# Expert passes of 32 rows in four column strips, three experts' rows at once, nine weight slots

## What is computed

```python
def hier_moe(x, w_group, b_group, w_router, b_router, w_gate_up, w_down):
    ...   # top-1 of 4 groups, then top-2 of the 8 experts in that group
    order = jnp.argsort(expert)
    ...
    def expert_block(a):
        xb, e = a
        gate, up = jnp.split(xb @ w_gate_up[e], 2, axis=-1)
        return (jax.nn.silu(gate) * up) @ w_down[e]
    ...   # sum of each token's two rows with their weights
```

## Time and profile before

| what | value |
|---|---|
| median of the runs shown | 2142.19 us |
| the profiled execution, its own time | 2152.84 us |
| its span, first to last instruction | 2150.9 us |
| TensorE (PE) busy | 1699.6 us, 79% |
| VectorE (DVE), ScalarE (ACT), POOL busy | 487.9, 324.3, 121.9 us |
| bytes read from and written to HBM | 551.57 MB, 52.01 MB |
| mean granted TensorE clock | 0.905 of full speed |

### The profile page before, as it was taken

The page is one execution under the profiler, slowest core; times in us unless marked ns, Lnnn a source line. Parts: engine busy times, 40 slices in busy tenths (PEclk is TensorE's granted clock), DMA queues, the critical chain, the costliest instruction groups (busy, mean ns, idle before and its releaser), DMA issues.

```text
span 2150.9 us, 25298 instructions
## 1 busy us (share of the span) xinstructions
PE 1699.6 (79%) x8325; PEld 783.4 (36%) x8326; DVE 487.9 (23%) x1022; ACT 324.3 (15%) x601; POOL 121.9 (6%) x147
## 2 busy tenths in 40 slices
PE   5988687687947888787887679989748788788682
PEld 3433233345432433333332334434523333233231
DVE  1679344320150101000000132120410000000003
ACT  3022334222020000001110220000200011010001
...
DMA  9951586685047596999999930201468899999995
GB/s 353 416 172 70 204 306 235 228 301 227 0 161 311 214 414 259 401 419 417 423 423 420 350 139 0 79 0 41 195 243 329 324 416 422 421 423 422 421 423 214
DMA packets 144964, 604.27 MB, mean 281 GB/s; under 512 B 15952, under 2 KB 18289, under 8 KB 128362
## 3 DMA queue, kind: packets, MB, share of 16 engines
...
HBM read 551.57 MB, written 52.01 MB: 281 GB/s over the span
## 4 chain that ended last, share of the span: by engine, by line
PE 63%; DMA 12%; DVE 10%; issue 7%; ACT 4%; POOL 1%; SPq 1%; ACTq 1%; DVEq 0%; POOLq 0%
PE ps L883 19%; PE ps L896 10%; PE ps L1008 8%; DMA ring<-in_w_gate_up_dram 5%; PE ps L578 5%; PE ps L594 3%; DMA ring<-in_w_down_dram 2%; PE ps L928 2%; PE ps L623 2%; PE ps L906 1%; DVE W L1483 1%; PE ps L940 1%; PE ps L520 1%; PE ps L496 1%; PE ps L718 1%
## 5 line engine op out<-in xcount | busy, mean ns | idle before, releaser
L883 PE MATMUL ps<-ring,W 128*64 128x512 f32 x2048 | 474.6, 615 | 48.3 <-issue 33.2
L896 PE MATMUL ps<-ring,W 128*64 128x512 f32 x1024 | 263.1, 659 | 54.7 <-DVE W L1806 49.3
L883 PEld LDWEIGHTS ps<-ring,W 128*64 128x64 f32 x2048 | 175.8, 141 | 335.1 <-issue 335.1
L1033 ACT ACTIVATE W<-ps 128x512 f32<-128x512 f32 (+3 forms) x244 | 138.1, 579 | 899.1 <-PE ps L896 353.8
L1800 DVE TENSOR_TENSOR W<-W,ps 128x256 f32<-128x256 f32 x64 | 27.0, 422 | 788.9 <-ACT W L1334 788.9
L1008 PE MATMUL ps<-hT,ring 128*128 128x512 f32 x384 | 168.0, 597 | 0.0
L896 PEld LDWEIGHTS ps<-ring,W 128*64 128x64 f32 x1024 | 88.0, 151 | 188.3 <-issue 188.2
L1008 PEld LDWEIGHTS ps<-hT,ring 128*128 128x128 f32 x384 | 72.8, 191 | 94.5 <-issue 94.5
L623 PE MATMUL ps<-ring,hT 128*128 128x512 f32 x192 | 88.6, 618 | 1.9 <-DVE W L1498 1.9
L1334 ACT ACTIVATE W<-ps 128x256 f32<-128x256 f32 x64 | 24.6, 384 | 423.3 <-PE ps L883 423.1
L1483 DVE SCALAR_TENSOR_TENSOR W<-W,prm 128x512 f32<-128x512 f32 x116 | 85.3, 805 | 0.0
...
## 6 DMA issues: line engine op xcount, KB each, us to landing
ring<-in_w_gate_up_dram SPq DMA_DIRECT2D x128, 2048.0 KB, 15.8
...
W<-x_rows SPq DMA_DIRECT2D x32, 512.0 KB, 15.4
x_rows<-W ACTq DMA_DIRECT2D x128, 128.0 KB, 6.7
...
```

The lines of the kernel that those rows point to most:

```text
L883: x = mm(ps[CAP * z:CAP * z + CAP, 2 + j, :], xt[:, k, :], at[:, :, 256 * z:256 * z + 256], start=(k == 0), stop=(k == KD - 1))
L896: x = mm(ps[CAP * z:CAP * z + CAP, 5 + j, :], ht[:, k % 2, CAP * (k // 2):CAP * (k // 2) + CAP], ring[:, 3 * j + 2, at:at + 512], start=(k ...
L1033: return fn(out, src, ACT.Copy, **k)
```

## The change

- `CAP` is 32. `x_rows` has 33 blocks of 32 rows ahead of the further area (`NEAR`), and every pass, main or further, has the form of today's further pass: stationary operands of 32 rows, four column strips, moving pieces of 256, one transpose between, a copy of 128 columns. An expert with more than 32 rows has a further pass for each 32 beyond.
- The rows of three experts (96) are loaded and turned at once, on ACT's queue instead of SP's, into one tile instead of two, a group ahead.
- The ring has nine slots. The three new ones lie over `hT` and a part of `W`, which for that become one tensor `M_` with `Hb`; the work tiles of the stage move into `Hb` (and `xg2` into free rows of `X`), and the router's tables move within `W`. Slots 6 and 7 are loaded once the logits are done, slot 8 once the bounds are. Loads then run three experts ahead.
- A loop body has three experts; two are written out behind it. A result is stored by four DMAs of 32 KB.

```diff
-CAP = 64
+CAP = 32
...
-PAIRS = E // 2
+GROUPS = -(-E // 3)
+NEAR = (E + 1) * CAP
 XTRA = 2 * (2 * T // XC)
-XR = -(-(E * CAP + (XTRA + NB - 1) * XC) // P) * P
+XR = -(-(NEAR + (XTRA + NB - 1) * XC) // P) * P
...
 NSLOT = 6
+NRING = 9
...
+M_SLOT = (M_HT, M_HT + SLOT, M_HT + 2 * SLOT)
...
-        Hb = sb("Hb", [P, NT, D])
-        hT = sb("hT", [P, KD, T])
-        W = sb("W", [P, W_N])
+        M_ = sb("M", [P, M_W + W_N])
+        Hb = M_[:, M_HB:M_HT].rearrange("p (a b) -> p a b", a=NT)
+        hT = M_[:, M_HT:M_W].rearrange("p (c t) -> p c t", c=KD)
+        W = M_[:, M_W:M_W + W_N]
...
+        xg, xT = m(M_XG, D)[0:3 * CAP], m(M_XT, KD, 3 * CAP)
+        hh, hhT, yh = m(M_HH, 3, P), m(M_HHT, 3, 4, CAP), m(M_Y, 3, 256)
...
+        def slot(s):
+            return ring[:, s, :] if s < NSLOT else M_[:, M_SLOT[s - NSLOT]:M_SLOT[s - NSLOT] + SLOT]
...
-        AHEAD = 2
+        AHEAD = 3
...
-            def quad(q, last=False):
-                step(4 * q, 0, 2 * q, 0)
-                step(4 * q + 1, 1, 2 * q, 0, nxt=(1, q, 2 * q + 1))
-                step(4 * q + 2, 0, 2 * q + 1, 1)
-                step(4 * q + 3, 1, 2 * q + 1, 1, nxt=None if last else (0, q + 1, 2 * q + 2))
-
-            with eng.Fori(0, E // 4 - 1) as q:
-                quad(q)
-            quad(E // 4 - 1, last=True)
+            with eng.Fori(0, E // 3) as q:
+                for j in range(3):
+                    step(3 * q + j, j, q, more=True)
+            for j in range(E % 3):
+                step(E - E % 3 + j, j, E // 3)
...
+                    sp.dma_start(slot(3 * j + k).rearrange("p (k n) -> p k n", k=4), src).then_inc(
...
-                def rows_in(p, j):
-                    sp.wait_ge(M["xt_mm"], pdone(l, p - 2))
-                    sp.dma_start(xg[:, j, :], x_dram[bass.ds(P * p, P), :]).then_inc(x_in[j], 16)
-
-                def step(n, j, e, pair=None):
-                    sp.wait_ge(M["g0_mm"], done(l, n))
-                    part(e, j, 0)
-                    sp.wait_ge(M["gu_mm"], done(l, n))
-                    part(e, j, 1)
-                    if pair is not None:
-                        rows_in(*pair)
-                    sp.wait_ge(M["down_mm"], done(l, n))
-                    part(e, j, 2)
-
-                layer_wait(sp, l, "disp", 32 * NT)
-                rows_in(0, 0)
-                rows_in(1, 1)
-                step(0, 0, 2 * EG, pair=(2, 0))
-
-                def quad(q, last=False):
-                    step(4 * q + 1, 1, 3 * EG + q)
-                    step(4 * q + 2, 0, q + 1, pair=(2 * q + 3, 1))
-                    step(4 * q + 3, 1, EG + q + 1)
-                    step(4 * q + 4, 0, 2 * EG + q + 1, pair=None if last else (2 * q + 4, 0))
-
-                with sp.Fori(0, 6) as q:
-                    quad(q)
-                quad(6, last=True)
-                step(E - 3, 1, E - 1)
+                layer_wait(sp, l, "h_ok", NT)
+                layer_wait(sp, l, "lg_mm", 1)
+                part(2 * EG, 2, 0)
+                part(2 * EG, 2, 1)
+                layer_wait(sp, l, "bounds", 1)
+                part(2 * EG, 2, 2)
+
+                def step(q, i):
+                    n, e = 12 * q + i, EG * ((i + 3) % G) + 3 * q + (i + 3) // G
+                    for k, name in enumerate(("g0_mm", "gu_mm", "down_mm")):
+                        sp.wait_ge(M[name], done(l, n))
+                        part(e, i % 3, k)
+
+                with sp.Fori(0, 2) as q:
+                    for i in range(12):
+                        step(q, i)
+                for i in range(E - 3 - 24):
+                    step(2, i)
...
-                def gate_up(xt, j, half, signal):
+                def gate_up(xt, j, half):
                     for k in range(4 * half, 4 * half + 4):
-                        at = ring[:, 3 * j + half, D * (k % 4):D * (k % 4) + D].rearrange("p (g f) -> p g f", g=2)
-                        for z in range(2):
-                            x = mm(ps[CAP * z:CAP * z + CAP, 2 + j, :], xt[:, k, :], at[:, :, 256 * z:256 * z + 256],
+                        at = slot(3 * j + half)[:, D * (k % 4):D * (k % 4) + D].rearrange("p (g f) -> p g f", g=2)
+                        for z in range(4):
+                            x = mm(ps[CAP * z:CAP * z + CAP, 2 + j, 0:256], xt[:, k, :], at[:, :, P * z:P * z + P],
                                    start=(k == 0), stop=(k == KD - 1))
-                    x.then_inc(signal, 1)
-
-                def h_turns(src, j, signal):
-                    for k in range(2):
-                        x = tr(ps[:, 4 + 3 * j, P * k:P * k + P], src[:, P * k:P * k + P], ident)
-                    x.then_inc(signal, 1)
-
-                def down(ht, j, signal):
+                    return x
+
+                def h_turn(src, j):
+                    return tr(ps[:, 2 + j, 256:256 + P], src, ident)
+
+                def down(ht, j):
                     for k in range(FE // P):
-                        for z in range(2):
-                            at = D * k + 512 * z
-                            x = mm(ps[CAP * z:CAP * z + CAP, 5 + j, :], ht[:, k % 2, CAP * (k // 2):CAP * (k // 2) + CAP],
-                                   ring[:, 3 * j + 2, at:at + 512], start=(k == 0), stop=(k == FE // P - 1))
-                    x.then_inc(signal, 1)
-
...
+                def group_turns(q):
+                    pe.wait_ge(x_in, q * 16 + (16 * GROUPS * l + 16))
+                    pe.wait_ge(M["xa_ok"], gdone(l, q - 1))
+                    pe.wait_ge(M["xd_ok"], gdone(l, q - 1))
                     carry(pe)
+                    n = 3 * CAP
                     for k in range(KD):
...
+                        x = tr(ps[:, k // 4, n * (k % 4):n * (k % 4) + n], xg[:, k:D:KD], ident[0:n, 0:n])
                     x.then_inc(M["xt_mm"], 1)
 
...
+                def step(n, j, q, more=False):
+
+                    def landed(k):
+                        pe.wait_ge(slot_in[3 * j + k], q * 16 + (base_in[l][3 * j + k] + 16))
+
...
                     further(pe, l, n, one_pass, ways=(2, 2, 2, 2))
-                    pe.wait_ge(M["xa_ok"], pdone(l, p))
-                    pe.wait_ge(M["xd_ok"], pdone(l, p))
-                    pe.wait_ge(M["h_ok"], done(l, n - 2))
-                    xt = xT[:, lane, :, CAP * j:CAP * j + CAP]
-                    landed(j, 0, p)
+                    if j == 0:
+                        pe.wait_ge(M["xa_ok"], gdone(l, q))
+                        pe.wait_ge(M["xd_ok"], gdone(l, q))
+                    pe.wait_ge(M["h_ok"], done(l, n - 3))
+                    xt = xT[:, :, CAP * j:CAP * j + CAP]
+                    landed(0)
                     carry(pe)
-                    gate_up(xt, j, 0, M["g0_mm"])
-                    landed(j, 1, p)
+                    gate_up(xt, j, 0).then_inc(M["g0_mm"], 1)
+                    landed(1)
                     carry(pe)
-                    gate_up(xt, j, 1, M["gu_mm"])
-                    if nxt is not None:
-                        pair_turns(*nxt)
+                    gate_up(xt, j, 1).then_inc(M["gu_mm"], 1)
+                    if more and j == 2:
+                        group_turns(q + 1)
                     pe.wait_ge(M["h_ok"], done(l, n))
-                    pe.wait_ge(M["ht_ok"], done(l, n - 2))
+                    pe.wait_ge(M["ht_ok"], done(l, n - 3))
                     carry(pe)
-                    h_turns(hh[:, j, :], j, M["ht_mm"])
-                    landed(j, 2, p)
+                    h_turn(hh[:, j, :], j).then_inc(M["ht_mm"], 1)
+                    landed(2)
                     pe.wait_ge(M["ht_ok"], done(l, n))
-                    pe.wait_ge(M["y_ok"], done(l, n - 2))
+                    pe.wait_ge(M["y_ok"], done(l, n - 3))
                     carry(pe)
-                    down(hhT[:, j], j, M["down_mm"])
-
-                pair_turns(0, 0, 0)
+                    down(hhT[:, j], j).then_inc(M["down_mm"], 1)
+
+                group_turns(0)
                 each_expert(pe, step)
...
+                def rows_in(q):
+                    act.dma_start(xg, x_dram[bass.ds(3 * CAP * q, 3 * CAP), :]).then_inc(x_in, 16)
...
+                gates(l, "gate2", w(W_G2, D), w(W_G2S, D, rows=NS), 0)
+                layer_wait(act, l, "disp", 32 * NT)
+                rows_in(0)
...
+                def group_turned(q):
+                    act.wait_ge(M["xt_mm"], gdone(l, q))
+                    act.wait_ge(M["gu_mm"], done(l, 3 * q - 1))
                     carry(act)
-                    copy(flat(xT[:, lane, 0:4, :]), ps[:, 0, :]).then_inc(M["xa_ok"], 1)
-
-                def step(n, j, p, lane, nxt=None):
+                    copy(flat(xT[:, 0:4, :]), ps[:, 0, 0:12 * CAP]).then_inc(M["xa_ok"], 1)
+
+                def step(n, j, q, more=False):
...
+                    if more and j == 0:
+                        carry(act)
+                        rows_in(q + 1)
                     further(act, l, n, one_pass)
```

(20 more changed lines are left out.)

169 lines of the change are left out of this document (81 added, 88 removed).

## The result

The changed kernel takes 2230.99 us (median of 4 runs, 2224.38 to 2252.32) against 2143.42 us on the same chip: a ratio of 1.041, 95% interval 1.034 to 1.049. It is slower, and the forecast of 2101 us (2063 to 2134) missed by 130 us. The profiled execution is the slowest of the four (2252.32 us, span 2250.6 against 2150.9), so its stretches are about 20 us longer in sum than the median's.

The account below looks back on a forecast made before the run. The prediction took the expert stages to be bound by the transfer of weights, with four stalls. Its terms, 30 + 8 + 11 - 4 + 0 - 4 = 41 us, taken from the median of 2142.19, gave 2101 us, range 2063 to 2134.

Parts of the forecast that it names:

- C, the stalls: Transfer standing still behind experts with further passes: 18 us won in layer 0, 7 lost in layer 1, sum +11 us.
- Pass of 8.94 us: Time of one further pass on TensorE, read from the kernel before and used for all 41 passes.
- 2 us of issue per cluster, nothing ahead of it: TensorE's idle time between an expert's last further pass and its main pass: 2.04 us in the profile before.
- Main pass of 7.6 us: Time of an expert's 32-row main pass on TensorE after the change: 7.2 us plus a share of turns, 7.6 us.
- A, nine slots: Three more weight slots filled during the router, taking 15.1 us per layer off the saturated transfer: +30 us.
- B: Fewer rows moved but shorter store pieces in the expert stages: between -7 and +22 us, taken as +8.
- E and F: Moved and new waits around the expert stages, such as dispatch, row gathers and projection: 0 and -4 us.
- D, the tail of layer 1: From last weights landing to last product: 15 to 16 us against 8, -8; with layer 0's +4, sum -4 us.
- E, the dispatch at 0: Start of the expert stages: first slot +2 us per layer, dispatch ending 2 us later beside slot 8, together 0.
- Slower: the clock: Rival: TensorE in the expert stages partly at half clock; 2185 us if a third of its work is; chance 0.08.
- The passes get dearer: Rival: row gathers beside weights make each further pass 2.5 us dearer, 40 us in all; 2141 us, chance 0.14.
- It doesn't do what it says: Rival: the three new slots don't fill ahead of the stage because SP waits earlier; 2131 us, chance 0.03.

Follow-up runs that it names:

- e2: The kernel before without its further passes (rows of an expert beyond 64 left out): 2069.5 us, ratio 0.962.
- e13: Kernel before with nine slots, still 64-row main passes, loop body of three experts, a one-cell Silu heading each body, three row buffers: 2177.4 us, ratio 1.012.
- e15: Changed kernel with a one-cell Silu at the loop body's head and ten empty loop turns on TensorE behind each cluster of passes: 2302.3 us, ratio 1.069.
- e5: Changed kernel with a one-cell Silu on ACT at the head of the loop body, so the table is loaded there: 2182.9 us, ratio 1.012.
- e1: Changed kernel without its further passes (rows of an expert beyond 32 left out): 2012.7 us, ratio 0.939.
- e18: Changed kernel without further passes, weights loaded two experts ahead instead of three, third set of slots not filled during the router: 2030.8 us, ratio 0.941.
- e12: Changed kernel with a one-cell Silu at the body's head and TensorE's four nested pass loops of two made two of four: 2182.8 us, ratio 1.013.
- e16: The kernel before with a one-cell Silu on ACT at the head of its loop body: 2145.0 us, ratio 0.997.

## Why the prediction was wrong

*The step that failed is C, the stalls.* "The later experts with one or two passes are covered by two experts of weights in the ring" did not hold. It forecast 54 us of stalls and -4 of tails for 41 passes; they cost 218 us. For the kernel before it had 65 us, and e2 shows 78. The way to count was near for 14 passes and off by a factor of four for 41. Nearly the whole miss lies there, since the terms that don't hang on passes came out (below). The durations in it were read where TensorE had a backlog:

- *Pass of 8.94 us.* It holds at full clock and away from the body's first expert: 896.13 to 905.83 us is one pass and its way out. At expert 3 a pass took 11.9 and 10.6 us, and four passes 47 us from 714.10 to 761.3 instead of 35.8. The table load (1.28 us) is new in passes because the body now begins at each third expert and ACT's load stands at the first Silu of the body. Before it fell only into main passes, because none of the experts at the head of a body of four has over 64 rows, which is chance. The Trainium skill (ScalarE activation tables: per-element evaluation and per-set limits, "Table sets in the compiler and the runtime") says that loads are placed per block, and the rows agree: 20 + 14 loads are the 20 main passes at position 0 of the looped bodies and the 14 passes that fall there by the rows per expert. The diff had it: a loop body's first Silu moved.
- *2 us of issue per cluster, nothing ahead of it.* Before, down's products of 3.67 us and more were queued while the queue walked into the passes (0.3 us of idle time at 112 turns). A down of 1.93 us no longer hides it: 48.5 us of idle time ahead of the turns (0.6 us in e13, with the long down), 87 us ahead of gate and up. The number of clusters tripled too, from 9 to 27, as the forecast's 54 us of issue had it; that sum was used for the clock's rival alone. e15 prices a us of gap at 1.26 us.
- *Main pass of 7.6 us.* Right at full clock: 7.3 to 7.5 us a step at 751 to 766 us of e5. At half clock behind a gap and with the table load it was 10.3 us (988.59 to 998.91 us of the changed kernel).
- *Expert 3 was to start at 681 us and the stall to stand at 702 to 720.* It started at 714 and the stall stood at 730 to 765, 35 us. Three mains at the start took 40 us, not the 29 of the forecast: half clock, and two gaps of 4.64 and 5.84 us when the body's code ran first, with three packets of the instruction queue between 680 and 705 us.

```profile
686.55 6.22 PE L891 MATMUL ps<-ring,M 128*32 128x256 f32 x64 [4.64 <-issue]
...
702.45 1.93 PE L891 MATMUL ps<-M 128*32 128x256 f32 x16 [5.84 <-issue]
```

*A, nine slots, was right*: 14.8 us per stage in the traces of e1 and e18, for 15. The 4 to 6 MB ahead of the stages came as well, as the three tiles of the new slots, 6.3 MB.

*B.* The row of +8 us already holds the rows of 27 more passes, so it can't be compared with kernels that have none. Without them the same count gives, as an estimate, 16.5 MB less, 39 us at 0.42 MB/us, or 19 if a store with shorter pieces saves nothing; the middle is 29. Measured: the stages are 997 us in e2 and 968 in e18, 29 us. With A and the -4 of E and F that is 55 us, against 57 between e1 and e2 (59 by the stages). That the middle was hit so closely is luck, since e18 differs from e2 in the whole shape of its passes and not only in its rows.

*D, the tail of layer 1*, was forecast at 15 us behind the last landing; it was 42 us (2174 to 2216.5): two clusters and two main passes, with gaps behind the clusters of 2.81 and 2.72 us and products at 5.37 and 5.16 us:

```profile
2173.16 5.37 PE ps L891 x64
2182.04 2.81 issue
...
2204.99 2.72 issue
2207.71 5.16 PE ps L891 x64
```

*E, the dispatch at 0*: the first gate and up came at 671.63 us, 20 us late. Little of that can be the change's: the changed kernel's variants have it at 654.16 (e1) to 668.29 us (e12), and the kernel before, at 651.33 in its own profile, at 665.63 with the Silu (e16). These are single executions, and the clock ahead of the stage differs from one to the next (0.91 from 500 to 520 us in the kernel before, 0.67 here, 0.50 in e16).

*The rivals.* "Slower: the clock" was on the right side, with 2185 us and a chance of 0.08, and its point of decision was near: 27% of TensorE's work at half clock, and what was measured, 125 of the 689 us that lie between its two sums, is 18%. (Its price at a third, 43 us, should be 46: 907 + 230 - 1091.) It didn't decide alone: gaps and table loads, which that rival left as they were, made up as much. Its row (a wait and then 0.50) was the right one; the waits that matter were not those for weights but those at the passes. "The passes get dearer" had the right place and the wrong reason: the gathers landed in time, as all but 0.1 of the 48.6 us ahead of the turns is issue. What I counted against the clock, that a full TensorE keeps it up, needs a TensorE without gaps, and these are what the change made. "It doesn't do what it says" didn't come: the slots filled.

The signs named in advance: 6720 records and 328 turns came as said; the pass wasn't near 9 us and so C was wrong by its own test; the clock in the stages was 0.86 and 0.89, not mostly 0.5. The stall of layer 0 came later and longer, and layer 0's last down ended at 1268, not 1171. The saturated rate, the sign for B, stands at its limit: where the share is 1.02 it is 409 to 412 GB/s with passes, 413 and 414 in e1 from 660 to 1130 and 1560 to 1960 us, and 413 and 422 in e2.
